# A block of mLSTM mixer and SwiGLU: feed-forward sums on VectorE, down weights streamed in an 11-slot ring, last product by rows

## The reference, cut to what matters

```
h = rms_norm(x) * (1 + sc1) + sh1
x = x + g1 * mlstm_mixer(h)                  # 4 heads, 1024 tokens, model width 1024
h = rms_norm(x) * (1 + sc2) + sh2
gate, up = split(h @ w_gate_up)              # w_gate_up: 1024 x 5632
x = x + g2 * ((silu(gate) * up) @ w_down)    # w_down: 2816 x 1024
out = rms_norm(x) * final_norm_w
```

## Time and profile before

| | us |
|---|---|
| median of 3 runs (lowest, highest) | 1226.18 (1226.14, 1229.16) |
| the profiled execution: its time | 1227.45 |
| the profiled execution: its span | 1225.6 |
| PE busy in the span | 1120.4 |
| DVE busy in the span | 733.1 |
| POOL busy in the span | 491.2 |
| ACT busy in the span | 430.6 |

### The profile page before, as it was taken

One profiled execution on the slowest core, in us unless ns is written; L12 is line 12 of the kernel. 1 busy time (PEld: TensorE's weight loads), 2 busy tenths in 40 slices (PEclk: granted clock), 3 DMA queues, 4 the chain that ended last, 5 costly groups with the idle time before them and its releaser, 6 DMA issues.

```text
span 1225.6 us, 16783 instructions
## 1 busy us (share of the span) xinstructions
PE 1120.4 (91%) x6060; PEld 962.6 (79%) x6060; DVE 733.1 (60%) x1064; ACT 430.6 (35%) x818; POOL 491.2 (40%) x342
## 2 busy tenths in 40 slices
PE   4899999999997999988999999999999568699995
PEld 3788899899896998877888888888888346587884
DVE  7956618238259636456555655565554499684564
ACT  6663222122223323344333333433332313243452
POOL 3432303103236326436344453444544799560002
PEclk9899999999999999999999999999999799899998
DMA  8315415224245312113224332233329822232333
GB/s 348 137 57 190 142 36 155 90 86 141 75 119 180 131 41 95 53 52 130 74 90 129 112 112 79 85 129 112 112 78 365 330 69 69 57 99 80 101 95 145
DMA packets 54936, 146.43 MB, mean 119 GB/s; under 512 B 5944, under 2 KB 6584, under 8 KB 53840
## 3 DMA queue, kind: packets, MB, share of 16 engines
q1 hardware_dynamic: 54160, 143.35, 35.2%
q0 software_dynamic: 704, 2.13, 0.5%
HBM read 116.83 MB, written 28.62 MB: 119 GB/s over the span
## 4 chain that ended last, share of the span: by engine, by line
PE 73%; DVE 16%; DMA 4%; issue 3%; ACT 2%; SPq 0%; POOL 0%; DVEq 0%; POOLq 0%; ACTq 0%
PE OP L1900 21%; PE OP L1676 15%; PE O L1900 11%; PE DC L1900 4%; PE ST L1900 4%; PE AD L1900 3%; DVE dwL L1558 3%; PE O L1676 3%; PE ST L1676 3%; DVE daL L1556 3%; PE AD L1676 2%; DMA daF<-act_mid 2%; DVE acc L1206 2%; PE DC L1676 1%; DVE wsL L1504 1%
## 5 line engine op out<-in xcount | busy, mean ns | idle before, releaser
L1676 PE MATMUL OP<-wH,hH 128*128 128x256 f32 x640 | 184.5, 288 | 3.3 <-DVE hL L1337 2.9
L1676 PE MATMUL OP<-wH,hL 128*128 128x256 f32 x640 | 180.9, 283 | 0.0
L1676 PE MATMUL OP<-wL,hH 128*128 128x256 f32 x640 | 180.8, 283 | 0.0
L1504 DVE TENSOR_TENSOR wsL<-raw,wsH 128x512 fp32r<-128x512 f32 x66 | 90.4, 1395 | 87.0 <-ACT wsH L1040 87.0
L1556 DVE TENSOR_TENSOR daL<-daF,daH 128x512 fp32r<-128x512 f32 x77 | 83.2, 1081 | 81.2 <-ACT daH L1100 81.2
L1676 PEld LDWEIGHTS OP<-wH,hH 128*128 128x128 f32 x640 | 122.4, 191 | 6.5 <-issue 3.2
L1676 PEld LDWEIGHTS OP<-wL,hH 128*128 128x128 f32 x640 | 122.5, 191 | 0.0
L1676 PEld LDWEIGHTS OP<-wH,hL 128*128 128x128 f32 x640 | 122.4, 191 | 0.0
L1900 PE MATMUL OP<-tH,wsH 128*128 128x512 f32 x264 | 104.0, 394 | 4.9 <-DVE c L1529 4.9
L1100 ACT CAST daH<-daF 128x512 fp32r<-128x512 f32 x77 | 47.7, 619 | 167.0 <-DMA daF<-act_mid 134.1
L1900 PE MATMUL OP<-tH,wsL 128*128 128x512 f32 x264 | 103.7, 393 | 0.0
(11 more groups left out here) (288 smaller groups left out, 2872.9 us busy)
## 6 DMA issues: line engine op xcount, KB each, us to landing
raw<-w_units SPq DMA_DIRECT2D x76, 512.0 KB, 4.0
daF<-act_mid SPq DMA_DIRECT2D x77, 256.0 KB, 2.6
ada<-ada_rest SPq DMA_DIRECT2D x64, 256.0 KB, 2.8
wd<-w_units SPq DMA_DIRECT2D x11, 1024.0 KB, 9.9
ada<-ada_first SPq DMA_DIRECT2D x8, 1024.0 KB, 9.9
act_mid<-actp SPq DMA_DIRECT2D x11, 512.0 KB, 2.8
act_mid<-s SPq DMA_DIRECT2D x11, 512.0 KB, 5.1
act_mid<-s SPq DMA_DIRECT2D x22, 256.0 KB, 4.1
```

The costliest lines, as they stand in the source:

```text
L1504: nc.vector.tensor_tensor(wsL[n % 2][i][:], src, wsH[n % 2][i][:].bitcast(F32), ALU.subtract).then_inc(c_L, 1)
L1676: ins = nc.tensor.matmul(out_ap, lhs[a], rhs[b], start=(n == 0 and i == 0), stop=(last and i == 2))
```

## The change

- `up_sum` of units 1 to 21 and `act_sums` move from GpSimd to DVE, at written places in its order. Unit 0 stays on GpSimd.
- The sums of the down weights no longer wait for the second stage. For each of 22 chunks (256 columns of two 128-row blocks), SP loads 512 KB into `wst` (`load_chunk`, 1 KB pieces), DVE makes the four sums in three instructions (`chunk_sums`), and SP stores 512 KB to DRAM, `down_mid` (`save_chunk`). This goes on beside the first stage.
- `wd`, `load_down`, `scale_down` and the ring of 6 are gone. A ring of 11 slots takes for each step two loads of 256 KB, operand and weights side by side (`dF`), and is split by one cast (`step_high`) and one subtraction (`step_low`) of 128x1024.
- g2 is no longer put on the weights but on the results. Finished products are copied out of PSUM by ACT (`down_copy`) or added by DVE (`down_add`) into `sA` and `sB`, some BEHIND = 17 steps behind the start of the product in the order of the splits; `down_rest` multiplies by g2 and adds to `x3`.
- The last product runs by rows (`down_last`): all 11 steps of row 0, then of row 1, 2 and 3. `last_rows`, `final_variance` and `finish` follow row by row. GpSimd has no part in the end. A half of the squares of rows 4 to 7 is made earlier (`half_ready`).
- Between the mixer's output product and the feed-forward part, DVE's `norm_row` of a token row is put behind the next output tile.

```diff
-POOL_ROWS = (4, 5)
 DOWN_SEQ = (1, 2, 5, 6, 7, 3, 4)
-RING = 6
+CHUNK = 256
+BEHIND = 17
...
+        def step_free(eng, s):
+
+            if s >= NG:
+                eng.wait_ge(d_mm, 4 * (s - NG + 1))
...
             for n in range(NF - 2):
-                if n >= 2 and n % 2 == 0:
-                    save_act(n // 2 - 1)
+                if n >= 2:
+                    save_chunk(n - 2)
+                    if n % 2 == 0:
+                        save_act(n // 2 - 1)
                 load_up(n + 2)
                 if n >= 2 and n % 2 == 0:
                     save_sums(n // 2 - 1)
+                if n:
+                    load_chunk(n - 1)
             end = NF - 1
+            save_chunk(NF - 4)
+            load_step(0)
             save_act(NG - 2)
...
+            load_chunk(NF - 3)
             save_sums(NG - 2)
...
+            for s in range(1, 6):
+                load_step(s)
+            save_chunk(NF - 3)
+            load_chunk(NF - 2)
+            for s in range(6, 9):
+                load_step(s)
+            load_step(9)
+            save_chunk(NF - 2)
+            load_chunk(NF - 1)
+            for t in range(4):
+                load_x(t, (end, 7))
+            for t in range(4, NT):
+                load_x(t, (end, 3))
             save_act(NG - 1)
...
+            sp.wait_ge(c_L, 7 * NF)
+            sp.dma_start(fw[:], final_w.to_broadcast([P, D])).then_inc(fw_in, 16)
+            load_step(10)
             save_sums(NG - 1)
...
+            save_chunk(NF - 1)
+            for s in range(NG, STEPS):
+                load_step(s)
...
+            def step_high(s):
+
+                g = s % NG
+                step_free(act, s)
+                act.wait_ge(d_in[g], 32 * (s // NG + 1))
+                nc.scalar.copy(dH[g][:], dF[g][:]).then_inc(d_H, 1)
...
+            def chunk_sums(n):
+
+                dve.wait_ge(t_in, 32 * n + 32)
+                nc.vector.tensor_tensor(wst[:, 0:2, :], wst[:, 1:4:2, :], wst[:, 0:2, :],
+                                        ALU.subtract).then_inc(t_ok, 1)
...
+            def step_low(s):
+
+                g = s % NG
+                dve.wait_ge(d_H, s + 1)
+                nc.vector.tensor_tensor(dL[g][:], dF[g][:], dH[g][:].bitcast(F32), ALU.subtract).then_inc(d_L, 1)
...
+            norm_row(NT - 1)
             add_c11(0)
             low(TR_AFTER[1])
             add_c11(1)
             low(TR_AFTER[2])
             low(TR_AFTER[3])
+            up_sum(1, 5)
             low(TR_AFTER[5])
+            up_sum(1, 6)
+            up_sum(1, 7)
             low(TR_AFTER[6])
+            up_sum(1, 3)
...
                 if n == 1:
+                    for q in SUM_SEQ:
+                        up_sum(2, q)
                     for q in L_SEQ:
                         up_low(2, q)
                 else:
                     for q in (6, 3, 4):
                         up_low(n + 1, q)
+                    if n % 2 == 0:
+                        act_sums(n // 2 - 1)
                     if n < NF - 2:
+                        for q in (5, 6):
+                            up_sum(n + 2, q)
                         for q in (2, 1, 5):
                             up_low(n + 2, q)
                 add_c22(n)
                 if 2 <= n < NF - 2:
+                    up_sum(n + 2, 7)
                     up_low(n + 2, 7)
                 add_c11(n + 1)
+                if n == NF - 2:
+                    step_low(0)
                 add_c12(n)
...
+                elif n < NF - 2:
+                    up_sum(n + 2, 3)
+                chunk_sums(n - 1)
...
             products(NF - 1)
...
+            act_sums(NG - 1)
+            for s in range(4, 8):
+                step_low(s)
+            chunk_sums(NF - 1)
+            for s in range(8, STEPS):
+                step_low(s)
+                m, at_end = divmod(s - BEHIND, NG)
+                if m in (1, 4) and at_end == 0:
                     for r in range(4):
...
+                        down_add(m, r)
...
+            for r in range(4):
+                down_add(5, r)
+            for r in range(4):
+                down_rest(5, r)
+            for t in range(4):
+                final_variance(t)
+                if t:
                     finish(t - 1)
...
+                if t == 2:
+                    last_rows(0)
+            finish(3)
+            for r in range(1, 4):
+                final_variance(3 + r)
+                last_rows(r)
+                finish(3 + r)
+            final_variance(NT - 1)
             finish(NT - 1)
...
+            def down_last(r):
+
+                pe.wait_ge(d_add, 4 + r + 1)
+                for g in range(NG):
+                    if r == 0:
+                        pe.wait_ge(d_L, STEPS - NG + g + 1)
+                    ins = down_three(DOWN_X[r], g, r, False, g == NG - 1)
+                ins.then_inc(d_mm, 1)
```

More of the change, by code:

```diff
@@ L278, in build @@
         a_sum, a_saved, s_saved = sem("a_sum"), sem("a_saved"), sem("s_saved")
[L279 to L282, removed]
+        t_in, t_ok, t_saved = sem("down_sum_in"), sem("down_sum"), sem("down_sum_saved")
+        d_in = [sem(f"down_in{g}") for g in range(NG)]
+        d_H, d_L, d_mm, d_cp, d_add, d_x = (sem(f"down_{n}") for n in ("H", "L", "mm", "copied", "added", "x"))
+        f_out, half_ok = sem("f_out"), sem("half_ok")
         def slot(k):
@@ L554, in _ @@
+            for s in range(6, 9):
[7 more added lines that the diff above has]
+                load_x(t, (end, 3))
             save_act(NG - 1)
-            for t in range(4, NT):
-                load_x(t, (up_mm, UP_AT[end, 4] + 1))
-            load_act(6)
-            load_act(7)
+            sp.wait_ge(c_L, 7 * NF)
@@ new lines, in _, with down_add @@
+            DOWN_ROWS = {1: (0, 0, sA), 4: (1, 1, sB), 5: (0, 1, sA)}
+            ADD_AT = {1: 0, 4: 1, 5: 2}
+            def down_add(m, r):
+                n = 4 * ADD_AT[m] + r
+                bank = (DOWN_X if m == 4 else DOWN_Y)[r]
+                v = DOWN_ROWS[m][2][r]
+                dve.wait_ge(d_cp, {1: 0, 4: 4, 5: 8}[m] + r + 1)
+                dve.wait_ge(d_mm, 4 * (NG * m + NG - 1) + r + 1)
+                nc.vector.tensor_tensor(v[:], v[:], bank[:], ALU.add).then_inc(d_add, 1)
@@ L1660, in _ @@
-            for t in range(4, NT):
-                add_down(6, t - 4)
-                if t > 4:
-                    row_variance(2 * NT + t - 1, 2 * NT + t - 1)
-                if t > 5:
-                    finish(t - 2)
-            row_variance(3 * NT - 1, 3 * NT - 1)
-            finish(NT - 2)
+            act_sums(NG - 1)
[4 more added lines that the diff above has]
+                step_low(s)
+                m, at_end = divmod(s - BEHIND, NG)
+                if m in (1, 4) and at_end == 0:
+                    for r in range(4):
+                        down_add(m, r)
+                if m in (1, 4) and at_end in (1, 2, 3, 4):
+                    down_rest(m, at_end - 1)
+                if m == 4 and at_end in (7, 8, 9, 10):
+                    half_ready(at_end - 3)
@@ L1944, in up_product, with down_three @@
                 ins.then_inc(up_mm, 1)
+            def down_three(bank, g, r, first, last):
+                return chained(bank[:], tuple(d[g][:, 0, r * P:(r + 1) * P] for d in (dH, dL)),
+                               tuple(d[g][:, 1, :] for d in (dH, dL)), first, last)
             def down_step(s):
@@ L1969, in _ @@
                     down_step(q - 6)
-            for s in range(2, STEPS):
+            for s in range(2, STEPS - NG):
                 down_step(s)
+            for r in range(4):
+                down_last(r)
 def kernel(x, c, ada_w, ada_b, ml_w_in, ml_b_if, ml_norm_w, ml_w_out, gdn_w_in, gdn_conv_w, gdn_a_log, gdn_dt_bias,
```

421 lines of the change are left out of this document (197 added, 224 removed).

## The result

The changed kernel takes 1167.87 us in the median (1165.25 to 1171.11, 4 runs), beside 1227.43 for the kernel before (4 runs): a ratio of 0.9515, 95% interval 0.9485 to 0.9545. The forecast was 1164.0 us. The profiled execution took 1169.03 us with a span of 1167.2.

The account below looks back on a forecast made before the run. Bound taken: the second stage's start waits for 11 MB of `wd`, GpSimd's scaling and sums, and a DVE slowed by these. 1225.6 - 57.4 - 4.5 - 2 + 2 = 1163.7 span, 1164 forecast; range 1155 to 1172 (0.66).

Parts of the forecast that it names:

- The second stage, -57.4: Steps 2 to 76 take 261.4 us, need 204.0 at PE's pace; the excess of 57.4 us was to go.
- The turn, +2 in the sum: Start of second stage: loads and splits in time by narrow margins; 2 us added for margins failing or a half-clock product.
- Rival A: Queue late at the turn, moving 285 GB/s: 5 to 20 us lost, 1170 to 1185; chance 0.18 together with D.
- The first stage, -2: Three gaps near the stage's start change, steady units cost nothing: 2 us saved, bounds -6 and +5.
- (a): Start of first stage: `up_sum(1, 3)` ahead of `add_c22(0)` makes PE's 0.96 us gap at 539.09 grow by 0.6.
- (b): Unit 2's four sums ahead of its first subtraction: gap of 0.69 us at 548.20 becomes about 2.5, perhaps with half clock.
- (c): PE's 3.90 us gap at 582.31, ended by `add_c22(2)`, goes with the half-clock product after it: -6.4 us.
- rival B: DVE's order holds PE in the steady units: 1185 to 1200 at 1 us over; chance 0.06 in part, 0.02 gain gone.
- The tail, -4.5: From PE's last matmul to the span's end: 9.9 to 10.1 us instead of 14.6.
- The steady steps, 0: Second stage: 512 KB per 2.72 us, 193 GB/s at a share of about 0.74, costs nothing, with 0.8 to 3 us cover.
- Rival C: Pairs of 256 KB loads do not overlap, a step takes 5.2 us: +164, about 1328; slower (C or more of B) 0.05.
- Rival D: The turn's stall was `x3` and the stores, not `wd`; some 15 us stay, 1180; chance 0.18 together with A.

Follow-up runs that it names:

- experiment 9: Kernel before with GpSimd's 22 scalings of the down weights by g2 left out (factor missing in the result): 1198.38 us, ratio 0.9771.
- experiment 4: Kernel before with only the sums of weights of units 1 to 21 and sums of results moved from GpSimd to VectorE: 1213.12 us, ratio 0.9893.
- Experiment 1: Changed kernel with the `x3` rows and final weights loaded behind steps 22 to 42, not ahead of step 10: 1161.43 us, ratio 0.9469.
- experiment 2: Changed kernel with two subtractions of unit 2 put ahead of its four sums on VectorE: 1165.03 us, ratio 0.9495.
- experiment 5: Changed kernel with the sums of weights of units 1 to 21 and sums of results back on GpSimd: 1173.14 us, ratio 0.9566.
- Experiment 3: Changed kernel with the last product run step by step over all four rows, not by rows: 1179.5 us, ratio 0.9617.
- experiment 7: Changed kernel with a third, unused load of 256 KB for each of steps 11 to 76: 1180.1 us, ratio 0.962.
- experiment 8: Changed kernel with the third, unused 256 KB load a step and BEHIND = 11 instead of 17: 1170.97 us, ratio 0.9541.

## Why the prediction came out as it did

By its own sum, against the profiled execution: 1225.6 in the span, less 57.4, less 2.6 for the first stage (step 2 starts at 947.02, not 949.64), plus 8.3 at the turn, less 6.7 for the tail, makes 1167.2, which is the span.

**The second stage, -57.4: right.** From 982 us to the end PE has no gap. Two of its parts were tried alone: half of it goes with the scalings (experiment 9), 12.9 us with the sums, by the timelines mostly through a wait in GpSimd's order that the prediction did not name (experiment 4). These two overlap, since both end with GpSimd done sooner. What part `wd`'s transfer has was read from the full queue in experiment 9 and not tried by itself.

**The turn, +2 in the sum: too small, it is +8.3.** The step that failed is "step 10 lands by 964 and is split by 966.5": its cast began at 968.06 and it was split at 970.4. Three things made that. The 4.75 MB were reckoned at 410 GB/s, done by 959 to 961; from 950 to 963 us the queue moved 373 GB/s in the mean, with `fw` in it too, and the store landed at 964.4. `load_step(10)` waits for just this landing before it is issued, so the load's 3.6 us came behind it, while the sum let both share the queue. And PE was 2.6 us early, so step 10 was due at 968.8 and not 971.4. Rival A was thus right in kind and at the low end of its 5 to 20 us, but not by its own reason: the queue was far from its 285 GB/s. Experiment 1 shows that the order makes the loss: same bytes, the store lands in 3.1 us and not 11.5, no gap. There too SyncE waits for the landing, so it is the backlog ahead of the store that the wait makes dear. A run with the rows of `x3` in their place and only the wait taken away was not made.

**The first stage, -2: right in the sum, -2.6.** Of these, 0.8 us lie ahead of the stage (its first matmul at 506.49, not 507.25) and are within the scatter of that point; the stage itself gives 1.9. (a) The gap went from 0.96 to 1.32, less than the 0.6 us more that was reckoned. (b) 2.00 us for about 2.5, with a half-clock product, some 3.5 us in all (3.8 by experiment 2, 0.3 of them at 582). (c) "This gap goes" failed: it fell from 3.90 to 1.45. From the weights to `add_c22(2)` it was 3.2 us, as reckoned (3.0), but the weights were cast from 578.3 on and not 1.2 us earlier than before (576.25); SyncE asked for them 0.8 us later, not earlier, behind a store of results that came 2.4 us later (569.13 for 566.77), for (a) and (b) had put PE off, which the forecast counted for PE's need alone; and they took 1.3 us longer to come. The half-clock product behind the gap did vanish. The steady units have no gap, so rival B fell; the subtractions are at 0.685 us (0.963 and 1.439 before, sums and `raw`), and experiment 5 shows this to be due to the sums' engine.

**The tail, -4.5: too small, it is -6.7.** The chain of operations was as reckoned; what lies behind the last of them is 3.0 us, not the 5.1 taken over from before. Experiment 3 puts 7.9 us on the order by rows.

**The steady steps, 0: right.** Rival C fell, loads of 256 KB back to back do overlap: 192 GB/s ran at a share of 0.60 (0.74 was estimated), and 289 GB/s were carried at 0.90 without a wait of PE (experiment 7, 1050 to 1075 us). (256 KB is a quarter of the 1 MB of `wd`'s loads, not the half that the prediction says.) The condition that held `down_add(1)` behind step 28 has a cover that experiments 7 and 8 measured: it costs nothing at this load, and 9 us when a third load comes with it. Rival D fell as well, since the stall did go; though the `x3` rows it named were what cost the 8 us that stayed.

## What to carry to other kernels

Where one engine issues all DMAs in order, look for a wait on a store's landing between loads that the next products need. Here it lasted some 11 us behind 4 MB of loads and 3.1 without them: move what isn't needed yet behind the wait. Price an instruction on a helper engine by what is queued behind its wait, not by its own length: here one wait of 12.54 us held 16 scalings.

## What was not expected of the hardware

A gap ahead of a product did not always cost the clock, and its length alone does not tell. In the changed kernel, behind gaps of 1.32 and 1.45 us, at 538.72 and 582.42, the matmuls followed at 0.23 us; behind 2.00 us, at 549.17, they were 0.42 us apart until 552.3, and behind 3.48 us, at 976.95, until 982.7. In the kernel before, two gaps of nearly one length had it both ways, 2.57 us ahead of 988.63 and 2.56 us ahead of 994.19 (columns as in the earlier trace rows, the granted clock stands third from the end):

```profile
988.63:991.50 2.87, 2.87 (x12) 2.15 (x12) 2.87 (x2) 1.14 (x2) 2.87 (x2) 1.00 0.26 101
994.19:997.20 3.01, 3.01 (x7) 2.43 (x8) 3.01 (x2) 1.14 (x2) 3.01 (x2) 0.50 0.00 0
```

So taking away a gap near 2 us can save more than the gap itself (some 3.5 us in experiment 2, for 2.00).

The page's 5.1 us for a load of 256 KB from `w_units`, beside 2.7 and 2.9 from `act_mid` and `down_mid`, is not a property of the source: 22 of the 33 are asked for before 981 us, beside a busy queue. The DMA view of the changed kernel, 970 to 1000 us and, behind the "...", 1060 to 1090 us:

```profile
dF<-w_units SPq DMA_DIRECT2D x11, 256.0 KB, 6.1
...
dF<-w_units SPq DMA_DIRECT2D x7, 256.0 KB, 3.0
```
